# Beginning the expert gathers of a PEER layer when half of the heads have been searched

## The reference, cut to what matters

```
q = (x @ w_q).reshape(T, 8 heads, 2, 128)
s = einsum('thcd,hcnd->thcn', q, sub_keys)        # 8 x 2 lists of 128 scores per token
s1, i1 = top_k(s[:, :, 0], 16)
s2, i2 = top_k(s[:, :, 1], 16)
top_s, top_pos = top_k(s1[..., :, None] + s2[..., None, :], 16)   # per head
expert_idx, gates = ..., softmax(top_s)           # 8 heads x 16 picks = 128 rows per token
act = gelu(einsum('thkd,td->thk', u[expert_idx], x))
out = einsum('thk,thkd->td', gates * act, v[expert_idx])
```

## Time and profile before

| | before |
|---|---|
| time, median of 3 runs | 2249.93 us (2246.06 to 2255.07) |
| the profiled execution | 2251.75 us, its span 2249.8 us |
| DVE busy | 1456.2 us (65%) |
| PE busy | 1518.9 us (68%) |
| POOL busy | 984.5 us (44%) |
| moved by DMA | 761.66 MB, of which 536.94 MB by the gathers |

### The profile page before, as it was taken

How to read it: one execution, slowest core, us unless ns; L and a number is a source line. 1 busy time by engine, 2 the same in 40 slices (tenths; PEclk the granted TensorE clock), 3 DMA queues, 4 the chain that set the end, 5 groups by cost and what they waited for, 6 DMA issues and landing times. The chain is left out here.

```text
span 2249.8 us, 17182 instructions
## 1 busy us (share of the span) xinstructions
PE 1518.9 (68%) x5314; PEld 877.5 (39%) x5314; DVE 1456.2 (65%) x3153; ACT 332.2 (15%) x786; POOL 984.5 (44%) x1043
## 2 busy tenths in 40 slices
PE   8989500277666549875773988465766655889997
PEld 6547500132234235433531643253522222555453
DVE  1133899878687875789787578877887666243101
ACT  1121100011111111111211111111310000123101
POOL 0000377677665555776456477643455441000000
PEclk9979855599876669997766998776578778888998
DMA  8326899999999999999999999999899999663771
GB/s 261 122 37 215 298 410 409 408 391 409 401 389 396 405 405 387 405 409 391 403 399 404 397 396 410 382 399 389 311 357 399 399 398 397 219 241 113 245 278 56
DMA packets 268531, 761.66 MB, mean 339 GB/s; under 512 B 21310, under 2 KB 46605, under 8 KB 267802
## 3 DMA queue, kind: packets, MB, share of 16 engines
q0 software_dynamic: 147456, 536.94, 60.9%
q1 hardware_dynamic: 120986, 223.64, 28.1%
HBM read 757.88 MB, written 2.62 MB: 338 GB/s over the span
## 5 line engine op out<-in xcount | busy, mean ns | idle before, releaser
L902 POOL DMA_INDIRECT ROWS<-in_peer_u,IDX x512 | 485.5, 948 | 458.9 <-DVE ROWS L947 266.8
L947 DVE SCALAR_TENSOR_TENSOR ROWS<-ROWS,XP 128x1024 f32<-128x1024 f32 x512 | 607.4, 1217 | 57.0 <-DMA ROWS<-in_peer_u,IDX 49.0
L902 POOL DMA_INDIRECT ROWS<-in_peer_v,IDX x512 | 488.9, 955 | 307.1 <-DVE XP L951 114.7
L951 DVE SCALAR_TENSOR_TENSOR XP<-ROWS,GATE,XP 128x1024 f32<-128x1024 f32 x316 | 406.1, 1285 | 193.0 <-DMA ROWS<-in_peer_v,IDX 188.9
L285 PE MATMUL bank<-ring,XT 128*128 128x512 f32 (+6 forms) x928 | 400.5, 590 | 57.6 <-DMA ring<-in_ffn_w_up 30.3
L285 PE MATMUL bank<-ROWS,DG 128*128 128x512 f32 x774 | 368.3, 633 | 91.2 <-DMA ROWS<-in_peer_v,IDX 85.9
L285 PEld LDWEIGHTS bank<-ring,XT 128*128 128x128 f32 x928 | 187.1, 211 | 250.2 <-issue 181.9
L285 PEld LDWEIGHTS bank<-ROWS,DG 128*128 128x128 f32 x774 | 153.5, 203 | 298.9 <-issue 180.6
L285 PE MATMUL bank<-XT,ring 128*128 128x128 f32 (+2 forms) x1504 | 196.0, 294 | 20.7 <-DMA ring<-in_w_in 18.9
L285 PEld LDWEIGHTS bank<-XT,ring 128*128 128x128 f32 (+1 forms) x1504 | 188.5, 198 | 31.7 <-DMA ring<-in_w_in 19.9
L368 POOL TENSOR_TENSOR stat<-stat,CN 128x1 f32<-128x1 f32 x6 | 3.3, 548 | 341.5 <-DVE stat L1750 137.1
(11 more groups left out here) (384 smaller groups left out, 1495.0 us busy)
## 6 DMA issues: line engine op xcount, KB each, us to landing
ring<-in_peer_w_q SPq DMA_DIRECT2D x16, 2048.0 KB, 13.8
ring<-in_ple_w_gate SPq DMA_DIRECT2D x10, 2048.0 KB, 19.1
ring<-in_ffn_w_gate SPq DMA_DIRECT2D x8, 2048.0 KB, 15.3
ring<-in_ffn_w_up SPq DMA_DIRECT2D x7, 2048.0 KB, 19.1
ring<-in_a_w_in SPq DMA_DIRECT2D x6, 2048.0 KB, 11.0
ring<-in_w_in SPq DMA_DIRECT2D x6, 2048.0 KB, 24.6
ring<-in_ffn_w_down SPq DMA_DIRECT2D x6, 2048.0 KB, 30.2
ROWS<-in_peer_u,IDX POOLq DMA_INDIRECT x512, 12.4
```

The lines of the kernel that those rows point to most:

```text
L902: G.indirect_dma_start(ROWBUF[slot(n, c)][:, :], None, tables[table], bass.IndirectOffsetOnAxis(IDX[:, tt, c:c + 1], axis=0)).then_inc(row ...
L947: V.scalar_tensor_tensor(row, row, 1.0, XP[:, :], ALU.mult, ALU.mult, accum_out=ACTV[:, tt, c:c + 1]).then_inc(row_used, 1)
L951: V.scalar_tensor_tensor(XP[:, :], row, gate, XP[:, :], ALU.mult, ALU.add).then_inc(row_used, 1)
```

## The change

Only the search of tile 0 in layer 0 changes. After groups 0 and 1 (lists 0 to 7, heads 0 to 3) `best_pairs(0, 0)` is done at once, before groups 2 and 3. `gather_begin(0)` moves from behind the whole search to behind group 2. The cast of TI to TF is done for each half apart. All other calls of `picks` do both halves at the end, with the cast in two pieces of 128 columns in place of one of 256.

```diff
             def picks(tt):
 
+                early = l == 0 and tt == 0
                 for g in range(4):
+                    if g == 2 and early:
+                        pick_half(tt, 0)
                     name = f"s{tt}{g}"
                     gather_some(2)
                     V.wait_ge(bank_ready(name), turn(name))
...
                     best8(lambda k: SC[:, k, :], TV, TI, 8, lists)
-                V.tensor_copy(TF[:, :, :], TI[:, :, :]).then_inc(*tick("dve_step"))
-                V.wait_ge(*now("dve_step"))
-                best_pairs(tt, 0)
-                best_pairs(tt, 1)
+                    if early and g == 2:
+                        V.wait_ge(*nth("x_copied", 2))
+                        gather_begin(0)
+                for half in range(1 if early else 0, 2):
+                    pick_half(tt, half)
+
+            def pick_half(tt, half):
+
+                lists = slice(8 * half, 8 * half + 8)
+                V.tensor_copy(TF[:, lists, :], TI[:, lists, :]).then_inc(*tick("dve_step"))
+                V.wait_ge(*now("dve_step"))
+                best_pairs(tt, half)
...
                 picks(tiles[0])
-                if l == 0:
-                    V.wait_ge(*nth("x_copied", 2))
-                    gather_begin(0)
-                else:
+                if l == 1:
                     dve_sums(beside)
```

## The result

| | before | changed | ratio, 95% interval |
|---|---|---|---|
| median | 2246.06 us (5 runs) | 2235.49 us (5 runs, 2231.31 to 2236.88) | 0.9949 (0.9932 to 0.9966) |
| the profiled execution | 2251.75 us | 2236.88 us, its span 2234.9 us | |
| DVE, POOL busy | 1456.2, 984.5 us | 1451.2, 986.2 us | |

A forecast was written before the change was run, and what follows sets the result against it. DMA bytes, mostly gathers, were taken to bound 264 to 1900 us, with idle DMA room before. Row 30 landing at 302.1 instead of 308.5 gains 6.4 us: median 2249.93 - 6.4 = 2243.5, range 2235 to 2252 (forecast's own 2241 to 2246).

The forecast's parts named there:

- all later work moves by the same amount: Stages after pass 0, from 433 us on: the 6.4 us gained there carries unchanged to the kernel's end.
- First gather 13.5 us earlier: Search of tile 0: with half 0 merged early, the first gather is issued at 241.94 instead of 255.44 us.
- Group 2 without a wait: Search, after the early merge: group 2's scores already lie ready, so DVE's wait of 2.67 us is gone.
- Waits for rows, 4.0 us: DVE within the search: 3.2 us waiting for row 1 plus 0.8 for the next rows.
- the slow rival: Search: all 18 rows come at 3.14 us each, DVE waits 13 us, kernel 2.6 us slower, 2252.5; chance 0.11.
- the one without waits: Search: row 1 and followers land in time, resumption at 291.6, gain 10.4 us, time 2239.5; chance 0.16.
- 18 rows of 1.15 us in the search: DVE in the rest of the search: 18 rows add 20.7 us; search ends at 293.35, row 18 starts at 295.6.
- Row 30 lands 5.0 us after its issue: Behind the search: issued at 297.1, landed at 302.1 against 308.5 before, so pass 0 ends 6.4 us earlier.
- The rival by bytes: Transfers up to 302.1 us: counted in bytes the gain is half, 3.4 us, time 2246.5; chance 0.28.
- The turns between the queues: Gathers beside weight transfers: each DMA engine alternates between its queues, a packet of each, giving a row each 2.13 us.
- the order of issue: Alternative to alternating queues: a 2 MB weight piece goes ahead of row 1, 5 us more waiting, gain 1.4 us.
- Chances: Whole kernel, against a 0.5% threshold (11.2 us): 0.82 within, 0.13 faster, 0.05 slower.

The follow-up runs named there:

- begin_early: Changed kernel, but rows may be used right behind the merge of half 0, ahead of group 2; ratio 0.9995 to the kernel before, on an uneven chip.
- The second pair of profiles: Unedited changed kernel against the kernel before, both on the chip where gathers kept 410 GB/s through pass 0; ratio 0.9968.
- half_only_3: Against the kernel before: half 0 merged early, so gathers start early, but no row used within the search; ratio 0.9962 (even chip), 0.9997 (uneven chip, as half_only).
- rows_only: Kernel before with its old search order, but 12 rows used within the merge of half 1; ratios 1.0011, 0.9994 and 1.0002, uneven chips only.
- quarters_fill: Changed kernel with heads 0-1 merged behind group 0, 2-3 behind group 1, and two rows moved into the exponentials' wait; 0.9952 and 0.9968 to the kernel before.

## Why the prediction was right and wrong

Its direction and its mechanism up to the end of pass 0 were right. The step that failed is its last one, *all later work moves by the same amount*, from which the 6.4 us at the end of pass 0 became 6.4 us of the median. The runs show 7.5 us there and 10.3 at the end of the span, both counted in t, and 10.6 in the medians.

- *First gather 13.5 us earlier*: t = 29.8 against 43.4, 13.5. Group 2 without a wait, row 0 at t = 35.0 (242.47), as worked out: right.
- *Waits for rows, 4.0 us*: 3.44, where they were expected. Neither the lower bound (no wait) nor the 13 us of the slow rival came, so the measured gain of over 8.5 us came by another way than the prediction's case for it, the one without waits; begin_early shows that the waits are real and grow when nothing covers them.
- *18 rows of 1.15 us in the search*: mis-sized. From row 0 to row 18 went 46.01 us; less 2.29 for the resumption, 3.44 of waits and 21.57 of search, 18.7 us are left for 18 rows, 1.04 each. That a row between two steps also covers a gap that a step leaves at its end is the likely reason, not tested. Row 18 came at t = 81.0 in place of 83.5.
- *Row 30 lands 5.0 us after its issue*: mis-sized the other way. Counted back from 420.57 in steps of 1.28 it landed at 296.4, 6.4 us after 289.97. Both together: 7.5 us gained at the last row, where 6.4 stood.
- *All later work moves by the same amount*: it held over the next two v passes: in t, their first rows start 7.2 us (599.9 to 592.7) and 6.8 us (1002.3 to 995.5) earlier than before. At the first v row of the last pass it no longer held: 10.1 us (1452.5 to 1442.3). The second pair of profiles repeats this, 1452.9 against 1442.4, and half_only_3 too, 1442.1. It goes with the transfers of t = 1210 to 1270: 383 and 384 GB/s in the two traces of the kernel before, 398 in these three. Why they run fuller there no run tells; the prediction looked at nothing in layer 1. To the end of the span the gain in t is 10.3 us in the first pair, 8.4 in the second and 10.4 in half_only_3. The medians of the two pairs say 10.6 and 7.3. Together that makes some 8 to 10 us for the change.
- *The start of the search*: the profiled executions differ by 14.9 us in span, and 4.6 of them lie ahead of the search. This part goes with the granted clock in the mLSTM, and the changed kernel was seen with either clock. But the kernel before was never seen to start its search below 210.9, so that it is chance stays likely and not shown.
- *The rival by bytes*: 3.4 us forecast. At t = 90 the lead was 2.1 MB, which is 5.1 us at 410 GB/s, and the first v row came 7.5 earlier: it was sized too low, and bytes at that point don't tell all. From the first MAX8 to the first v row the kernel before moved 82.99 MB and the changed one 81.83, since fewer rows of the v pass were in by then: 1.2 MB, 2.8 us. In the pair on the even chip these were 82.99 and 82.18. It is not shown that this is all of the difference.
- *The turns between the queues*: they hold in the changed kernel. From 244 to 252 us, with both queues at work, gathers and weights took 551 packets each, 2.00 MB to 1.13, and row 1 didn't wait the 5 us more that the order of issue would have cost. Over 240 to 256, which has stretches without gathers, it was:

```profile
q0 software_dynamic: 954, 3.50, 56.0%
q1 hardware_dynamic: 1218, 2.81, 45.7%
```

- *Chances*: 0.82 on within 0.5% and 0.13 on faster. The first measurement fell at 0.51%, the later ones within. The chance for faster rested on the case without waits; the waits came, so that case is no account of the first measurement.

## What to carry to other kernels

Where DMA is saturated for most of the time, value a change by the idle DMA time it fills ahead of the saturated stretch (bytes by rate), not by how much earlier a transfer is issued; count also what is left idle later while slots stand full. Here that ranked the kernels on the even chip rightly (1.5, 2.1 and 2.9 MB, with 6.2, 6.9 and 9.1 us at the first v row), and was some 2 us too low for each. Don't carry a shift to the end of the kernel without a look at the later stages. Compare two profiles from a landmark at the start of the changed stage, since stages ahead of it can differ by several us with the same code. Put the first use of an early transfer behind work that covers its flight: in an engine's fixed order everything behind it waits with it.

## What the runs showed of the hardware

The kernel before took 2316 to 2318 us on three chips and 2246 us in the first measurement, 3% less. With the same code and the same order of gathers, DMA moved 410 GB/s over 320 to 420 us on the even chip and 379 on the uneven one shown above. Nothing in these runs tells why.

On such chips the changed kernel's two traces have some 4.1 us of stops of DVE within the search, at waits that the trace puts on nothing in the core or on "issue", and PE took 50.59 and 50.75 us where it took 45.59 for the same 408 matmuls. half_only (3.12 us) and begin_early (4.45 us) have such stops there too, the kernel before has none, rows_only and quarters_fill none of over 0.7 us. The cause stays open. The changed kernel's medians kept 3.0 and 5.6 us of gain there.
